# Depthwise convolution on a Trainium2 core: one of eight channel tiles moved from TensorE to VectorE

## The reference

```python
def conformer_conv(h, w_in, b_in, dw, dw_b, ln_g, ln_b, w_out, b_out):
    d = h.shape[-1]
    a, g = jnp.split(h @ w_in + b_in, 2, axis=-1)
    u = a * jax.nn.sigmoid(g)
    u = lax.conv_general_dilated(
        u, dw[:, None, :].astype(u.dtype), window_strides=(1,),
        padding=((CONV_WIDTH - 1, 0),),
        dimension_numbers=('NWC', 'WIO', 'NWC'),
        feature_group_count=d) + dw_b
    u = jax.nn.silu(layer_norm(u, ln_g, ln_b))
    return u @ w_out + b_out
```

## Time and profile before

| | |
|---|---|
| time, median of 3 runs | 1029.85 us |
| lowest and highest | 1028.05 and 1029.86 us |
| the profiled execution, its own time | 1031.6 us |
| its span in the trace | 1029.8 us |
| mean granted TensorE clock | 0.992 of full |
| VectorE busy share | 70% |

### The profile page before, as it was taken

The page is one execution under the profiler, slowest core; times in us unless marked ns, Lnnn a source line. Parts: engine busy times, 40 slices in busy tenths (PEclk is TensorE's granted clock), DMA queues, the critical chain, the costliest instruction groups (busy, mean ns, idle before and its releaser), DMA issues.

```text
span 1029.8 us, 16219 instructions
## 1 busy us (share of the span) xinstructions
PE 1013.2 (98%) x6608; PEld 889.5 (86%) x6608; DVE 719.0 (70%) x880; ACT 491.5 (48%) x559; POOL 108.3 (11%) x83
## 2 busy tenths in 40 slices
PE   8999999999999999999999999999999899999998
PEld 7997778899999888986899999887887689999996
DVE  5859657987677777854887766678776776445664
ACT  5555465554444345422554343445556665344441
POOL 1031000000110000225001000010001301000000
PEclk8999999999999998999999999999999999999999
DMA  8984345849888783596639887786551536665541
GB/s 299 371 290 137 130 142 188 287 159 345 272 300 275 265 292 116 164 293 177 219 111 346 284 280 271 261 284 209 206 183 63 170 117 212 197 203 174 194 164 42
DMA packets 119600, 223.77 MB, mean 217 GB/s; under 512 B 6575, under 2 KB 21105, under 8 KB 119537
## 3 DMA queue, kind: packets, MB, share of 16 engines
q1 hardware_dynamic: 117152, 214.97, 61.6%
q0 software_dynamic: 2256, 7.88, 2.4%
q10 hardware_dynamic: 128, 0.03, 0.0%
HBM read 217.17 MB, written 1.05 MB: 212 GB/s over the span
## 4 chain that ended last, share of the span: by engine, by line
PE 88%; DVE 6%; DMA 2%; ACT 1%; issue 1%; POOL 1%; SPq 0%; DVEq 0%; ACTq 0%; POOLq 0%
PE ps L461 83%; DMA ada_raw<-in_ada_w 2%; PE ps L817 1%; DVE lo L367 1%; PE ps L1111 1%; ACT aS L1956 1%; DMA X<-in_x 1%; DVE X L921 1%; DVE ada_acc L1134 1%; PE ps L537 1%; POOL aS L2395 1%; DVE stat L2295 1%; PE ps L950 1%; PE ps L1490 0%; PE ps L545 0%
## 5 line engine op out<-in xcount | busy, mean ns | idle before, releaser
L367 DVE TENSOR_TENSOR lo<-raw,hi 128x2048 fp32r<-128x2048 f32 x151 | 349.1, 2318 | 221.9 <-ACT hi L356 221.3
L356 ACT ACTIVATE hi<-raw 128x2048 fp32r<-128x2048 f32 x151 | 288.9, 1914 | 301.2 <-PE ps L461 272.8
L461 PE MATMUL ps<-hTh,hi 128*128 128x256 f32 x992 | 265.5, 286 | 0.3
L461 PE MATMUL ps<-hTh,lo 128*128 128x256 f32 x992 | 262.4, 283 | 0.0
L461 PE MATMUL ps<-hTl,hi 128*128 128x256 f32 x992 | 261.1, 283 | 0.0
L461 PEld LDWEIGHTS ps<-hTh,hi 128*128 128x128 f32 x992 | 182.2, 192 | 2.9 <-issue 2.4
L461 PEld LDWEIGHTS ps<-hTl,hi 128*128 128x128 f32 x992 | 181.7, 192 | 1.6 <-issue 1.2
L461 PEld LDWEIGHTS ps<-hTh,lo 128*128 128x128 f32 x992 | 182.2, 192 | 0.0
L461 PE MATMUL ps<-hi,hidh 128*128 128x512 f32 (+1 forms) x424 | 165.1, 389 | 0.0
L461 PE MATMUL ps<-hi,hidl 128*128 128x512 f32 (+1 forms) x424 | 163.6, 386 | 0.0
L461 PE MATMUL ps<-lo,hidh 128*128 128x512 f32 (+1 forms) x424 | 163.4, 385 | 0.0
(11 more groups left out here) (248 smaller groups left out, 871.1 us busy)
## 6 DMA issues: line engine op xcount, KB each, us to landing
raw<-in_mlp_w SPq DMA_DIRECT2D x64, 1024.0 KB, 5.2
ada_raw<-in_ada_w SPq DMA_DIRECT2D x44, 1024.0 KB, 7.4
raw<-in_w_in SPq DMA_DIRECT2D x20, 1024.0 KB, 7.9
raw<-in_w_ff_in SPq DMA_DIRECT2D x16, 1024.0 KB, 5.2
raw<-in_w_ff_out SPq DMA_DIRECT2D x16, 1024.0 KB, 5.3
raw<-in_attn_w_qkv SPq DMA_DIRECT2D x12, 1024.0 KB, 5.9
raw<-in_conv_w_in SPq DMA_DIRECT2D x8, 1024.0 KB, 6.3
taps<-u_pad SPq DMA_DIRECT2D x64, 71.0 KB, 6.0
```

Of the source, the lines that this page charges most:

```text
L356: nc.scalar.activation(hi[:, slot], raw[:, slot], ACT.Copy).then_inc(hi_made, 1)
L367: nc.vector.tensor_tensor(lo[:, slot], raw[:, slot], hi[:, slot].bitcast(F32), ALU.subtract).then_inc(lo_made, 1)
L461: return nc.tensor.matmul(o, lhs, rhs, start=start, stop=False, skip_group_check=True)
```

## The change

Tile 4 (the first of chunk 2) is no longer filtered by TensorE. VectorE does it by 31 operations of 128x256 on `u_pad`: the first is a multiply and add of a scalar per partition (with the bias), the other 30 are acc = u * tap + acc, into `cacc[:, 4]`, each waiting for the one before (`link`). They stand in five pieces in VectorE's order: 6 after `glu(2)`, 10 after `mid_unit(1, 0)` and its `ada_keep`, 4 ahead of `glu(3)`, 6 after the subtractions of tiles 0 and 1, and 5 after those of tiles 2 and 3. `mid_unit(1, 1)` moves from behind tile 1 to behind tile 5. GpSimd makes seven stationaries. The taps of tile 4 come as 31 rows by one more DMA, are transposed by one more small matmul and copied by VectorE into `pcol`. `spread(2)` still copies both tiles.

```diff
@@ -66,6 +66,9 @@
 N_CH = D // CH
 PARAMS["conv_dw"] = (256, TAP_GROUPS * N_CH)
 N_PCOL = 256 + TAP_GROUPS * N_CH
+PARAMS["vector_dw"] = (224, TAPS)
+K_VECTOR = 4
+K_TENSOR = (0, 1, 2, 3, 5, 6, 7)
 U_COLS = PAD + SEQ + 2
 REP_COLS = 4 * (TAP_GROUPS - 1) + SEQ
 
@@ -164,7 +167,7 @@
         ada_four = big("ada_four", 24576, [P, 4 * 512])
 
         prow = big("prow", 16384, [P, 2, P])
-        dwrow = big("dwrow", 24576, [P, 2, P])
+        dwrow = big("dwrow", 24576, [P, 3, P])
         wsrow = big("wsrow", 18432, [P, 4, P])
         gate = big("gate", 0, [P, 6, TT, 512])
         qT = big("qT", 24576, [P, 4, SEQ])
@@ -1385,6 +1388,7 @@
                 r = CH * (q % 4)
                 sp.dma_start(dwrow[r:r + CH, q // 4, 0:CH * n].rearrange("g (s c) -> g s c", c=CH),
                              conv_dw_2[0, 4 * q:4 * q + n].rearrange("s (g c) -> g s c", c=CH)).then_inc(dw_in, 16)
+            sp.dma_start(dwrow[0:TAPS, 2], conv_dw_2[0, :, P * K_VECTOR:P * K_VECTOR + P]).then_inc(dw_in, 16)
             mlp_sp(sp, 0, w_ff_in[0], w_ff_out[0], (o_lo, 8))
 
             def cin(c, h):
@@ -1418,7 +1422,7 @@
                 cout(c, 1)
             spread(2)
             spread(3)
-            mlp_sp(sp, 1, mlp_w1_2[0], mlp_w2_2[0], (conv_pe, KT))
+            mlp_sp(sp, 1, mlp_w1_2[0], mlp_w2_2[0], (conv_pe, len(K_TENSOR)))
             for c in range(6):
                 for h in range(2):
                     load(sp, U_QKV + 2 * c + h,
@@ -1592,9 +1596,10 @@
                                tail=TAIL_BANK[2] if c == 1 and h == 1 else None)
 
             def conv_taps():
-                pe.wait_ge(dw_in, 16 * TAP_GROUPS)
+                pe.wait_ge(dw_in, 16 * TAP_GROUPS + 16)
                 for g in range(2):
-                    last = nc.tensor.transpose(ps[:, 6, g * P:(g + 1) * P], dwrow[:, g], ident)
+                    nc.tensor.transpose(ps[:, 6, g * P:(g + 1) * P], dwrow[:, g], ident)
+                last = nc.tensor.transpose(ps[:, 6, 2 * P:2 * P + TAPS], dwrow[0:TAPS, 2], ident[0:TAPS, 0:TAPS])
                 last.then_inc(dw_tr, 1)
 
             square(U_OUT, 1, conv_taps)
@@ -1617,11 +1622,14 @@
 
                 pe.wait_ge(*taps_in(c))
                 for kk in range(2):
-                    pe.wait_ge(sel_made, 2 * c + kk + 1)
+                    if 2 * c + kk == K_VECTOR:
+                        continue
+                    n = K_TENSOR.index(2 * c + kk)
+                    pe.wait_ge(sel_made, n + 1)
                     for q in range(TAP_GROUPS):
                         for j in range(STRIPS):
                             last = mm(pe, ps[CH * j:CH * j + CH, 4 + c, kk * SEQ:(kk + 1) * SEQ],
-                                      dw_sel[:, kk, q, j], taps4[:, c % 3, kk, j, 4 * q:4 * q + SEQ], q == 0)
+                                      dw_sel[:, n % 2, q, j], taps4[:, c % 3, kk, j, 4 * q:4 * q + SEQ], q == 0)
                     last.then_inc(conv_pe, 1)
 
             def moments(c):
@@ -2141,6 +2149,7 @@
                 dve_step(dve, U_OUT + h)
             dve.wait_ge(dw_tr, 1)
             at, n = PARAMS["conv_dw"]
+            nc.vector.tensor_copy(par("vector_dw", 0, TAPS), ps[:, 6, n:n + TAPS])
             link(dve, nc.vector.tensor_copy(pcol[:, at:at + n], ps[:, 6, 0:n]))
             no_tap = CH * (TAPS % 4)
             nc.vector.memset(pcol[no_tap:P, at + n - N_CH:at + n], 0.0).then_inc(dw_ok, 1)
@@ -2188,25 +2197,46 @@
                         scalar=par("conv_b_in", 2 * c + i), in1=csg[:, c % 2, i], op0=ALU.add,
                         op1=ALU.mult).then_inc(u_ok, 1)
 
+            def vector_taps(first, past):
+
+                k = K_VECTOR
+                dve.wait_ge(u_ok, k + 1)
+                for s in range(first, past):
+                    x, ws = u_pad[:, k // 2 % 2, k % 2, s:s + SEQ], par("vector_dw", s)
+                    if s == 0:
+                        link(dve, nc.vector.tensor_scalar(cacc[:, k], x, ws, par("conv_dw_b", k), ALU.mult, ALU.add))
+                    else:
+                        link(dve, nc.vector.scalar_tensor_tensor(out=cacc[:, k], in0=x, scalar=ws, in1=cacc[:, k],
+                                                                 op0=ALU.mult, op1=ALU.add))
+
             for c in range(CHUNKS):
                 dve_step(dve, U_CIN + 2 * c)
+                if c == 3:
+                    vector_taps(16, 20)
                 glu(c)
+                if c == 2:
+                    vector_taps(0, 6)
                 dve_step(dve, U_CIN + 2 * c + 1)
                 if c < 3:
                     mid_unit(dve, c // 2, c % 2)
                 if c == 2:
                     ada_keep(dve, ADA_MID[0], 7)
+                    vector_taps(6, 16)
             dve.wait_ge(first_mean, 1)
             for k in range(KT):
-                if k < 2:
+                if k < 2 or k == K_VECTOR:
                     nc.vector.tensor_tensor(cacc[:, k], cacc[:, k], cmean[:], ALU.subtract).then_inc(cs_xc, 1)
                 else:
-                    dve.wait_ge(conv_pe, 2 * (k // 2) + 2)
+                    dve.wait_ge(conv_pe, sum(n // 2 <= k // 2 for n in K_TENSOR))
                     nc.vector.scalar_tensor_tensor(
                         out=cacc[:, k], in0=ps[:, 4 + k // 2, (k % 2) * SEQ:(k % 2 + 1) * SEQ],
                         scalar=par("conv_dw_b", k), in1=cmean[:], op0=ALU.add,
                         op1=ALU.subtract).then_inc(cs_xc, 1)
                 if k == 1:
+                    vector_taps(20, 26)
+                if k == 3:
+                    vector_taps(26, TAPS)
+                if k == 5:
                     mid_unit(dve, 1, 1)
             dve.wait_ge(cs_sum, 1)
             nc.vector.tensor_scalar(cvar[:], ps[:, 4, SEQ:2 * SEQ], 1.0 / D, EPS, ALU.mult,
@@ -2357,11 +2387,12 @@
             dw = par("conv_dw", 0, TAP_GROUPS * N_CH).rearrange("p (q g) -> p q g", q=TAP_GROUPS)
             s4 = sel.unsqueeze(1).unsqueeze(1).broadcast_to([P, TAP_GROUPS, STRIPS, CH])
 
-            def stationaries(k):
-                if k >= 2:
-                    pool.wait_ge(conv_pe, k - 1)
+            def stationaries(n):
+                k = K_TENSOR[n]
+                if n >= 2:
+                    pool.wait_ge(conv_pe, n - 1)
                 w = dw[:, :, STRIPS * k:STRIPS * (k + 1)].unsqueeze(3).broadcast_to([P, TAP_GROUPS, STRIPS, CH])
-                nc.gpsimd.tensor_tensor(dw_sel[:, k % 2], s4, w, ALU.mult).then_inc(sel_made, 1)
+                nc.gpsimd.tensor_tensor(dw_sel[:, n % 2], s4, w, ALU.mult).then_inc(sel_made, 1)
 
             mid_load(pool, 0, 1)
             stationaries(0)
@@ -2370,8 +2401,8 @@
             stationaries(2)
             stationaries(3)
             mid_load(pool, 1, 1)
-            for k in range(4, KT):
-                stationaries(k)
+            for n in range(4, len(K_TENSOR)):
+                stationaries(n)
 
             pool.wait_ge(ada_kept, event(8) + 2)
             pool.wait_ge(row_c_in, 16)
```

## The result

The changed kernel takes 1033.27 us (median of 12 runs, 1030.99 to 1035.31), the kernel before 1029.82 us beside it (12 runs, 1028.05 to 1030.29). The ratio is 1.0037, 95% interval 1.0027 to 1.0048: slower by some 3.5 us (by the interval 2.8 to 4.9). The forecast was slower, 1035.8 us, with a range of 1031.5 to 1037.4.

What follows compares the result with a forecast made beforehand. TensorE, busy for 98% of the span, was taken to bound the kernel. Shedding 3.5 us but delayed by held taps, the stage came to +4.8 us; the clock fall made it +6.0: 1035.8 us, range 1031.5 to 1037.4.

Steps and rivals of the forecast that it cites:

- The price of a tap: On VectorE, one linked multiply-add of 128x256 was to take 0.515 us, so 31 taps 16.0 us.
- Taps are held by GpSimd: In the convolution stage, VectorE operations with both inputs in SBUF stand still until GpSimd's operation is over, 1.9 us.
- glu(3): On VectorE, the products of chunk 3 were to be done at 472.2 against 464.7, 7.5 us late.
- The stand ahead of moments(0): TensorE was to stand from 471.04 to 475.8, 4.7 us, until VectorE had made tiles 0 and 1.
- the walk: VectorE's operations from glu(2) on, timed one by one with taps and GpSimd's holds, to find when later steps come.
- conv(3) waits 1.2 us for the spread: TensorE, ready at 483.1, was to wait another 1.2 us for the last DMA of spread(3), landed at 484.3.
- The clock falls: TensorE's clock was to drop to half from 475 on, during the stand, adding 1.2 us in all.
- the sum: The whole forecast for the run: +4.8 us without a clock fall, +6.0 us with it.
- The tail: Behind conv(3), 9.1 us of GpSimd operations hold VectorE; multiply-adds end near 495.2, last sum at 497.5 against 492.7.
- The small edits: One more transpose and one more copy of 31 columns near 200 us: between nothing and 0.7, taken as 0.1 us.
- The change does what it says: Rival: taps are not held by GpSimd, so the stage ends 2.6 to 3.5 us early, 1027; chance 0.11.
- Its turning point: At conv(3): the sign was to turn where the products of chunk 3 are some 4 to 5 us late.

Runs made afterwards that it cites:

- the kernel with late taps: Changed kernel, the 31 taps moved to 7 behind `ada_keep`, 2 behind glu(3), 6 behind tile 1, 16 behind tile 3; ratio 1.0004 or 1.0065, GpSimd's X operations early or late.
- the late taps with X early: Changed kernel with the 31 taps placed later and GpSimd's `row_c` and two X adds moved ahead of the convolution stage; ratio 1.0004 to the kernel before.

## Why the prediction was right, and where its size was off

- **The price of a tap**: 0.515 from the nearest rows, 0.517 measured. The 0.33 us, an estimate from the Trainium skill's page VectorE: DVE Perf Modes (section on the TRN2 errata), is not borne out by any tap of these traces.
- **Taps are held by GpSimd**: right. Expected to take 2.4 us when held, they took 2.0 to 2.1 in the changed kernel, and 2.5 beside the longer `row_c` and X adds. The run with 32-column stationaries shows that this alone turns the sign.
- **glu(3)**: expected 7.5 us late, came 6.7 late (470.5 on before's clock). The difference is in how a hold was counted: I added the stationary's 1.9 us to the held tap's own 0.5; the second and third stationary made their tap 2.02 and 2.10 us long, so they added 1.5 and 1.6. A hold replaces the operation's own time.
- **The stand ahead of moments(0)**: expected 4.7, is 4.65. It did not come from glu(3) itself but from what stands behind it on VectorE, the `lo` held to 3.96 us and then tiles 0 and 1, as the walk had it. The stationary that holds this `lo` ends at 468.44, on before's clock 473.1 as expected, so the error of glu(3) dropped out.
- **conv(3) waits 1.2 us for the spread**: not in the changed kernel, where the half clock had delayed conv(3) already; with the clock kept full it waits 1.29.
- **The clock falls**: right (0.52 and 0.50 from 469 to 476 us). By the sum it adds 1.2; the run with the extra matmuls shows 0.9.
- **The tail** is the step that failed in size: the part behind conv(3) would be 2.5 us longer than before's and is 0.75 longer. I had VectorE's last two taps, tile 4 and the first of the four multiply-adds of mid_unit(1, 1) held by four operations of GpSimd (9.1 us from 481.2), and the multiply-adds end near 495.2. That comes out only if each held operation's own length is added to its hold, as at glu(3). Without it they end at 481.2 + 9.1 = 490.3 and three multiply-adds of 0.79 later, at 492.7. The run with more matmuls, where the clock stayed full, shows this very sequence:

```profile
476.87 6.28 DVE L2211 SCALAR_TENSOR_TENSOR cacc<-u_pad,pcol,cacc 128x256 f32<-128x256 f32 x5
483.19 2.49 DVE L2230 TENSOR_TENSOR cacc<-cacc,cmean 128x256 f32<-128x256 f32 x1
...
485.99 4.84 DVE L1137 SCALAR_TENSOR_TENSOR ada_acc<-ada_raw,cond,ada_acc 128x512 f32<-128x512 f32 x4
```

  Two of the five taps, tile 4 and one multiply-add are held (2.22, 2.47, 2.49 and 2.48 us), and the end is at 490.83, on before's clock 493.7: later than 492.7, since GpSimd's own operations are lengthened to 9.5 us. Its part behind conv(3) is 0.95 us longer than before's, not 2.5. In the changed kernel the sequence was another. The last stationary waits for the end of conv(2), which the half clock put off to 478.94 (483.6 on before's clock, 481.2 in the walk). So the taps, done at 477.64, and tile 4, at 478.10, went clear of it, and all four multiply-adds were held instead (10.45 us, end at 489.94, on before's clock 494.6). That was no gain by itself, but conv(3) had started later too, and what was left was a wait of 0.48 us for tiles 6 and 7.

- **The small edits** were taken at 0.1 us; the third transpose alone costs 0.35.

In sum: -3.45 (expected -3.52), stand +4.72 (+4.7), clock and spread together +2.36 (+2.4), tail +0.75 (+2.5): 4.4 against 6.0, and 4.7 with the transpose. The run medians give 3.5, with an interval that takes in both.

- **The rivals.** "The change does what it says" is what happens with the holder taken away, though at 1.2 us faster by the medians and 1.9 in the stage, not 2.6 to 3.5: conv(3) then waits for the spread. Its turning point, products of chunk 3 some 4 to 5 us late, was named at the wrong place: they came 6.7 late and conv(3) did not wait for them. What decided was moments(0), the next thing on TensorE that needed VectorE.

## What to carry to other kernels

An idle hole of an engine is worth what the work put in it lasts beside its neighbours, not alone: look for what GpSimd does in the same microseconds, and give the held duration to each operation with both inputs in SBUF that meets it. Put filling work behind the operations that others wait for, never ahead of them, and move only as much as the holes take: 31 taps cost 3.5 us, 24 of the same taps in better places gained 1.4. When an engine is late at one point, ask again which of the later steps still meet each other: here the taps escaped and the multiply-adds behind them were caught. And when two operations take turns, count the hold in place of the held operation's own time, not on top of it.

## What the runs showed of the hardware beyond that

- The first tap is a `tensor_scalar` with one tensor input from SBUF. It too was held (2.07 us beside the stationary at 443.47, 0.40 us in the kernel with late taps, where nothing ran on GpSimd), though the rule that I took from the rows was "both inputs in SBUF". The Trainium skill, page SBUF — State Buffer, section "Who interferes with whom", lists `tensor_scalar` among the operations that can take the shared pair; the traces agree, also with 2.01 and 2.11 us for it in the kernels with more matmuls and with one tap.
- A GpSimd that has several operations queued and a VectorE with a row of linked taps take turns one for one: 2.49, 2.48 and 2.48 us for three taps in a row.
- The hold works both ways: with VectorE's `lo` beside it, `row_c` took 4.32 us and the X adds 4.4 each, against 2.38 and 2.4 in the earlier trace rows.
- The granted clock fell to half (1.2 GHz) in a stand of 4.65 us between two full stretches of matmuls, and in one of 6.75 us; it stayed full where 18 matmuls of 128 columns were put into that stand and left a wait of 0.34 us. The Trainium skill, page TensorE: Matmul & The Clock Gate, section on HAM oscillation, has waits between bursts throw the clock back; in these stands the trace agrees.
- The clock fall near 400 us does not come in every execution, and not with one length: before's profiled one has it for 6.8 us, those of ten experiments for 3.4, those of after and of the late taps with X early not at all. The runs of after lie in three groups, near 1031.3, 1033.3 and 1035.2 us, with mean granted clocks of 0.996, 0.995 and 0.993.
